# Score products from 32-row or 64-row slices of split q and k, in place of 128-row stacks read back from DRAM

## The reference

```python
# A: 4 heads, each with two components of 32 channels
sc = jnp.einsum("bqhcd,bkhcd->bhcqk", qblk, k).astype(jnp.float32) * scale
sc = jnp.where(kpos[None, :] <= qpos[:, None], sc, -jnp.inf)
p = jax.nn.softmax(sc, axis=-1)
pd = p[:, :, 0] - lam * p[:, :, 1]
# C: 4 heads of 64 channels, dilated windows, here as one softmax with a mask of log counts
sc = jnp.einsum("nbqhd,nbkhd->nbhqk", qb, k2).astype(jnp.float32) * scale
```

## Time and profile before

| | |
|---|---|
| median of three runs | 927.5 us |
| the profiled execution | 927.7 us, span 925.9 us |
| busy: TensorE / VectorE / ScalarE / GpSimd | 698.4 / 506.5 / 337.4 / 285.0 us |
| DMA queue of SyncE | 80.60 MB |
| DMA queue of GpSimd (gathers) | 67.12 MB |
| granted TensorE clock, mean | 0.873 of full speed |

### The profile page before, as it was taken

How to read it: one execution, slowest core, us unless ns; L and a number is a source line. 1 busy time by engine, 2 the same in 40 slices (tenths; PEclk the granted TensorE clock), 3 DMA queues, 4 the chain that set the end, 5 groups by cost and what they waited for, 6 DMA issues and landing times.

```text
span 925.9 us, 11484 instructions
## 1 busy us (share of the span) xinstructions
PE 698.4 (75%) x4171; PEld 565.0 (61%) x4171; DVE 506.5 (55%) x801; ACT 337.4 (36%) x731; POOL 285.0 (31%) x195
## 2 busy tenths in 40 slices
PE   4699999999778995994128750777646359979996
PEld 4599888888667774784014430554535246668885
DVE  5745864553557854343028860696844487665222
ACT  6523232322112122321006820676727366672111
POOL 4034445465345554261005201331131262000000
PEclk9699999999899998898558975889969578999999
DMA  7544678775768878646445423332314261522231
GB/s 233 187 146 136 188 232 272 257 232 172 242 209 282 303 261 286 193 160 237 114 138 171 173 91 129 127 104 67 109 56 151 88 179 49 70 1 94 101 104 69
DMA packets 87277, 148.44 MB, mean 160 GB/s; under 512 B 14131, under 2 KB 57955, under 8 KB 87222
## 3 DMA queue, kind: packets, MB, share of 16 engines
q1 hardware_dynamic: 68790, 80.60, 28.5%
q0 software_dynamic: 18432, 67.12, 21.7%
HBM read 124.47 MB, written 23.26 MB: 160 GB/s over the span
## 4 chain that ended last, share of the span: by engine, by line
PE 40%; DMA 31%; DVE 10%; SPq 6%; issue 5%; ACT 4%; POOL 4%; ACTq 0%; DVEq 0%; POOLq 0%
DMA ka_d<-KL 6%; PE ps L1779 6%; PE ps L1781 5%; PE ps L1780 5%; DMA kc<-in_cache_c_k 4%; DMA kc<-in_w_out 4%; DMA TMP<-gate_d 4%; PE ps L1840 3%; PE ps L1912 3%; PE ps L1913 3%; PE ps L1914 3%; DMA stack<-kc_d 3%; DMA stack<-ka_d 2%; DMA vc<-in_cache_c_v 2%; DMA kbuf<-in_cache_a_k,index 2%
## 5 line engine op out<-in xcount | busy, mean ns | idle before, releaser
L1779 PE MATMUL ps<-xh,wh 128*128 128x344 f32 x576 | 198.1, 344 | 9.1 <-DVE passing L1255 7.1
L1780 PE MATMUL ps<-xl,wh 128*128 128x344 f32 x576 | 188.2, 327 | 0.0
L1781 PE MATMUL ps<-xh,wl 128*128 128x344 f32 x576 | 188.0, 326 | 0.0
L1282 DVE TENSOR_TENSOR prod<-kbuf,qrep 128x1024 f32<-128x1024 f32 x64 | 87.6, 1368 | 86.6 <-DMA kbuf<-in_cache_a_k,index 83.6
L1779 PEld LDWEIGHTS ps<-xh,wh 128*128 128x128 f32 x576 | 112.0, 194 | 31.3 <-issue 21.3
L768 POOL DMA_INDIRECT kbuf<-in_cache_a_k,index x64 | 72.9, 1139 | 138.1 <-DVE sc L1284 131.7
L1780 PEld LDWEIGHTS ps<-xl,wh 128*128 128x128 f32 x576 | 112.4, 195 | 0.0
L1781 PEld LDWEIGHTS ps<-xh,wl 128*128 128x128 f32 x576 | 112.0, 194 | 0.0
L1807 PE MATMUL ps<-stack,stack 128*128 128x512 f32 (+3 forms) x96 | 35.7, 459 | 100.1 <-DMA stack<-ka_d 72.8
L776 POOL DMA_INDIRECT vbuf<-in_cache_a_v,index x64 | 67.6, 1056 | 130.9 <-PE ps L1740 115.8
L1045 ACT ACTIVATE E<-T,negmax 128x128 f32<-128x128 f32 (+7 forms) x96 | 73.6, 768 | 48.2 <-DVE negmax L1404 48.0
(11 more groups left out here) (262 smaller groups left out, 1149.4 us busy)
## 6 DMA issues: line engine op xcount, KB each, us to landing
wraw<-in_w_in SPq DMA_DIRECT2D x24, 512.0 KB, 7.8
gate_d<-passing SPq DMA_DIRECT2D x8, 516.0 KB, 6.8
TMP<-gate_d SPq DMA_DIRECT2D x8, 516.0 KB, 6.5
xraw<-in_x_prompt SPq DMA_DIRECT2D x8, 512.0 KB, 6.1
out<-nat SPq DMA_DIRECT2D x8, 512.0 KB, 5.5
stack<-kc_d SPq DMA_DIRECT2D x8, 512.0 KB
kc<-in_w_out SPq DMA_DIRECT2D x8, 512.0 KB, 11.6
x_res<-in_x_prompt SPq DMA_DIRECT2D x8, 512.0 KB, 4.1
```

Source lines behind the costliest of these rows:

```text
L1282: link(dve.tensor_tensor(prod[:], kbuf[n % 2][:], qrep[b % 2][:].unsqueeze(1).to_broadcast([P, CH, W_BR]), ALU.mult))
L1779: pe.matmul(pr, wh[t % 2][:, kt, :], xh[:, kt, cols], start=(kt == 0), stop=False)
L1780: pe.matmul(pr, wh[t % 2][:, kt, :], xl[:, kt, cols], start=False, stop=False)
L1781: ins = pe.matmul(pr, wl[t % 2][:, kt, :], xh[:, kt, cols], start=False, stop=(kt == KT - 1))
```

## The change

The stacks, their DRAM tensors, the stores and the loads are taken out. A pair's split halves stay in SBUF, and the scores read a head's own rows of them. The first pair keeps QH, QL, KH, KL; the second and fourth share four tiles `half0x`, the third has `half1x`, all where the stacks were. So the split of the second pair waits for the end of the projections (whose inputs lie there), and that of the fourth for the last score of head 3. Each component of an A head and each C head has three accumulated products, qh kh + ql kh + qh kl, over 32 or 64 rows; the product ql kl is left out. For an A unit both PSUM halves are awaited first, and the two components' products alternate. `v_c` is loaded at unit 10 rather than 34.

```diff
-        stack = [[at(f"stack{s}{i}", [P, S], F32R) for i in range(4)] for s in range(2)]
+        halves = [[at(f"half{s}{i}", [P, S], F32R) for i in range(4)] for s in range(2)]
...
+        pair = [[QH, QL, KH, KL], halves[0], halves[1], halves[0]]
...
             for step in range(PSTEPS + 8):
...
-                if step - 10 in SPLIT_AT and SPLIT_AT.index(step - 10) % 2:
-                    store_pair(0, SPLIT_AT.index(step - 10) // 2)
...
             sp.wait_ge(proj, ALL_CHUNKS)
...
-            load_stack(0, 0, FIRST, first_stack)
             sp.dma_start(mask_a[:], a["c_mask_a"]).then_inc(mask_in, 16)
-            load_stack(0, FIRST, S)
             gates_stored(sp)
             sp.dma_start(v_a[:], nat_out["va"]).then_inc(va_in, 16)
-            load_stack(1)
             sp.dma_start(mask_c[:], a["c_mask_c"]).then_inc(late_in, 16)
             for u in range(NU + 1):
                 h, q = UNITS[u] if u < NU else (8, 0)
-                if q == NQ - 1 and h in (0, 2, 4):
-                    store_pair(h // 2 + 1, 0)
-                    store_pair(h // 2 + 1, 1)
-                if q == 1 and h >= 1 and h + 1 < 8:
-                    load_stack(h + 1)
-                if u == UNITS.index((HA, 2)):
-
-                    sp.wait_ge(scored, ITEM_NO["s", UNITS.index((HA, 1)), 0] + 1)
+                if u == UNITS.index((1, 2)):
+
                     sp.wait_ge(split_done, 8)
                     sp.dma_start(v_c[:], nat_out["vc"]).then_inc(vc_nat_in, 16)
...
-                if p >= 1 and i == 0:
-                    pool.wait_ge(qk_out, stored(p - 1))
+                if p == 1 and i == 0:
+
+                    pool.wait_ge(proj, ALL_CHUNKS)
+                if p == 3 and i == 0:
+
+                    pool.wait_ge(scored, ITEM_NO["s", UNITS.index((HA - 1, NQ - 1)), 1] + 1)
...
-                high, low = ((QH, QL), (KH, KL))[i // 2]
+                high, low = pair[p][2 * (i // 2):2 * (i // 2) + 2]
...
-                    act.wait_ge(qk_out, stored(3))
+                    act.wait_ge(split_done, 16)
...
             def scores(u):
...
+                if q == 0 and h % 2 == 0:
+                    pe.wait_ge(split_done, 4 * (h // 2 + 1))
+                qh, ql, kh, kl = pair[h // 2]
+                qs = slice(q * P, (q + 1) * P)
+                n, d = (2, DKA) if h < HA else (1, DHC)
+                for c in range(n):
+                    keep_free(pe, ("s", u, c))
+                for k0 in range(0, w, 512):
+                    k1 = min(w, k0 + 512)
+                    for i, (a_, b_) in enumerate(((qh, kh), (ql, kh), (qh, kl))):
+                        for c in range(n):
+                            r = slice(64 * (h % 2) + d * c, 64 * (h % 2) + d * c + d)
+                            ins = pe.matmul(score_bank(("s", u, c))[:, k0:k1], a_[r, qs], b_[r, k0:k1],
+                                            start=(i == 0), stop=(i == 2))
+                            if i == 2 and k1 == w:
+                                ins.then_inc(scored, 1)
```

More of the change, by code:

```diff
@@ L304, in build @@
         sn_d = dram("sn_d", [2, NB, HCA])
-        qa_d, ka_d = dram("qa_d", [2, 4, 2, DKA, S]), dram("ka_d", [2, 4, 4, DKA, S])
-        qc_d, kc_d = dram("qc_d", [2, 2, 2, DHC, S]), dram("kc_d", [2, 2, P, S])
         x_d, xs_d = a["x_prompt"][0], a["x_sample"].rearrange("b t d -> (b t) d")
@@ L343, in build @@
         misc_out = sem("misc_out")
-        qk_out = sem("qk_out")
-        first_stack = sem("first_stack")
-        stack_in = [sem(f"stack_in{i}") for i in range(2)]
         va_in, vc_nat_in = sem("va_in"), sem("vc_nat_in")
@@ L440, in build @@
         EARLY_MIX = 2
[L441 to L447, removed]
         def keep_free(eng, it):
@@ L554, in _ @@
             sp.dma_start(cs[:, 0:2, :], a["state_conv"][0][:, 1:3, :]).then_inc(misc_out, 16)
[L556 to L567, removed]
             turn_no = [0]
@@ L638, in _ @@
             sp.wait_ge(proj, ALL_CHUNKS)
[L640 to L662, removed]
             def load_wo(k):
@@ L1794, in scores @@
                 w = (q + 1) * P
-                sl = stack[h % 2]
-                if u == 0:
-                    pe.wait_ge(first_stack, 16 * 4)
-                if u == FIRST // P or (q == 0 and h >= 1):
-                    pe.wait_ge(stack_in[h % 2], stacked(h))
-                for c in range(2 if h < HA else 1):
-                    it = ("s", u, c)
-                    keep_free(pe, it)
-                    out = score_bank(it)
-                    for k0 in range(0, w, 512):
-                        k1 = min(w, k0 + 512)
-                        if h < HA:
-                            ins = pe.matmul(out[:, k0:k1], sl[2 * c][:, q * P:(q + 1) * P], sl[2 * c + 1][:, k0:k1],
-                                            start=True, stop=True)
-                        else:
-                            pe.matmul(out[:, k0:k1], sl[0][:, q * P:(q + 1) * P], sl[1][:, k0:k1], start=True, stop=False)
-                            ins = pe.matmul(out[:, k0:k1], sl[0][:, q * P:(q + 1) * P], sl[2][:, k0:k1],
-                                            start=False, stop=True)
-                    ins.then_inc(scored, 1)
+                if q == 0 and h % 2 == 0:
[14 more added lines that the diff above has]
+                                ins.then_inc(scored, 1)
             def turn(u):
```

## The result

The changed kernel takes 836.3 us (median of four runs, 834.7 to 838.4), beside 927.2 us (924.6 to 928.8) for the kernel before on the same chip: a ratio of 0.902, 95% interval 0.899 to 0.906. A median here is of all runs of a kernel, a ratio and its interval of its fast runs alone, without those over 1.5% above its fastest. The forecast was 837 with a range of 806 to 880. The sum came out; its terms did not, and most of what follows is about that. The profiled execution took 834.8 us, with a span of 833.0 against 925.9.

The account below looks back on a forecast made before the run. The prediction saw TensorE 40% and DMA 31% of the wait chain, DMA mostly the split q/k round trip through DRAM, with VectorE binding attention between stalls. 9 + 32 + 31.5 + 10 + 21 - 13 = 90.5 off 927.7 gives 837, range 806 to 880.

Parts of the forecast that it names:

- The wait for vc, 9: End of the projections: without stores queued ahead, vc lands at the median and TensorE's 11.42 us wait goes; gain 9.
- The start, 32: Projections to unit 3: mask_a no longer waits behind KL's store and the first stack; u=3 moves from 487.87 to 456.
- Units 3 to 16, 31.5 less 7: Early A heads: 90.7 us fall to 59.2 at the free pace of 4.55 a unit, before costs of added products.
- Before unit 36, 10: C heads: the 10.14 us idle goes because v_c and a gate load both come earlier; 0 if the gate load stays late.
- Units 43 to 48, 21: C heads: 50.05 us against 19 for five free units; of 31 lost to w_out, a stall of 10 stays.
- The added products, 13: Scores: row slices overlap; exposed cost 3 in A, 6 in C, 4 for the banks; bounds 0 and 66.
- The 4 for the common wait for both banks: A units: the first product waits until VectorE has read both banks of the unit before; cost 4, 24 without cover.
- Row slices: Rival, score products: slices run one after the other, 42 us of TensorE work in place of 16.8; 866 us, chance 0.10.
- this change from slices to full rows: Rival, 64 units: each change of shape drains TensorE, 128 changes of 0.16 us add 20; 857 us, chance 0.08.
- the other transfers: Rival: gate loads and w_out stay late, slowed by the gathers rather than the stacks; 874 us, chance 0.14.
- the signs named as right: Attention: first mask some 15 us after projections, u=16 some 73 and u=32 some 152 after u=0, masks idle only for ScalarE.
- the signs named as wrong: Components over 0.2 us apart, masks mostly awaiting scores, load waits over 10 us, or granted clock near 0.5 through A heads.

Follow-up runs that it names:

- The first experiment: Changed kernel with the two stores of the split q (QH, QL) back on SP's queue ahead of the last vc loads; 858.5 us, ratio 0.923.

## Why the prediction was right, and which of its terms were not

*The wait for vc, 9.* The first experiment shows the mechanism. The stretch gave 15.6: the 11.42 us that TensorE waited are gone, and the other 4.2 lie within the spread of this stage between profiles of the same code. So 9, of at most 11.4, was near. With the round trip left in place it would have been worth 3.2.

*The start, 32.* Mis-sized, 40.1. The prediction kept three times of the trace before, and each fell. The last gate store, at 431.82, waits for VectorE's last step on its tile, and that ended 4.1 us after the last projection product, because VectorE had work on the samples, from 426.94 to 430.33, ahead of its last three steps on the tile; now it ends 2.1 after. The store took 2.56 us to issue, now 0.32. And mask_a lands in 4.16, not 8.2. VectorE's last step on the tile before the change; its like now starts at 413.60:

```profile
431.28 0.51 DVE L1255 SCALAR_TENSOR_TENSOR passing<-passing,ps 128x344 f32<-128x344 f32 x1
```

Thus 7 us from the last projection product to the first mask, where "some 15" was forecast.

*Units 3 to 16, 31.5 less 7.* 25.3 against 24.5, but by luck: both parts were too large. The free pace of 4.55 did not come; 65.5 us are 5.04 a unit, near the 4.96 of heads 2 and 3 that the prediction had as a bound. And the added products do not cost 7 here: without the two products with low halves the stretch takes 65.0. What holds the pace at 5.04 is not settled. The load of v_c ahead of the gate load cost nothing: it landed in 5.5.

*Before unit 36, 10.* The idle time did go, but 3.2 came of it, since unit 34 now takes 12.3 us where it took 5.4. The step that failed is "both come earlier, so 10 goes": it did not ask what the earlier gate load sets in motion. Before, GpSimd waited 20.89 us for that load and began its recurrence step and the split of the fourth pair at 683.57, behind the samples' last steps that stand in unit 34. Now it begins at 583.20, beside them. In units 32 to 36 VectorE runs the same instructions for the same units, and is busy 20.99 us where it was busy 14.13 (rows below); five short ones in unit 34 make up 7.0 of it. The longest of these, before and after, then GpSimd before and after:

```profile
667.54 0.19 DVE L1459 TENSOR_TENSOR w<-us,pT 128x32 f32<-128x32 f32 x1
```
```profile
586.70 2.38 DVE L1402 TENSOR_TENSOR w<-us,pT 128x32 f32<-128x32 f32 x1
```
```profile
683.57 2.37 POOL L848 TENSOR_TENSOR xb<-xb,TMP 128x1024 f32<-128x1024 f32 x1 [20.89 <-DMA TMP<-gate_d]
```
```profile
586.67 2.35 POOL L759 TENSOR_TENSOR half<-qc,half 128x1024 fp32r<-128x1024 f32 x1
```

Unit 34 takes 5.3 us in the kernel before with its stores moved as well, and 11.1 to 12.8 in all the others that have the samples' last steps there. No run keeps GpSimd idle in that unit, so this is read from the traces. Units 32 to 36 and 43 to 48 (length, busy us of PE, PEld, DVE, ACT, POOL, clock, DMA), before and after:

```profile
657.93:685.59 27.66, 11.59 (x70) 9.35 (x69) 14.13 (x35) 9.05 (x21) 5.01 (x2) 0.69 0.31 94
712.11:762.16 50.05, 20.37 (x97) 16.54 (x97) 28.23 (x64) 25.93 (x41) 23.28 (x10) 0.66 0.43 127
```
```profile
575.01:599.49 24.48, 14.50 (x81) 11.71 (x81) 20.99 (x35) 10.52 (x25) 11.77 (x6) 0.80 0.20 65
628.39:664.88 36.49, 24.63 (x105) 18.92 (x105) 29.22 (x64) 24.88 (x41) 24.54 (x10) 0.67 0.44 130
```

*Units 43 to 48, 21.* 13.6. "Five free units are 19" is false: the pace of 3.79 was taken from units 36 to 43, which have none of the samples' last steps, and VectorE alone was busy 28.23 of the 50.05, so no more than 22 could go. "A stall of 10 stays, from w_out's refills" named the wrong wait. The refills land in 3.8 and ScalarE waits 1.4 for them; what stays is VectorE's own work, a good part of it beside GpSimd's.

*The added products, 13.* Too large by some 5, an estimate from the ledger and the run without low products. They overlap and are covered in A, as forecast: there both low products together are worth 1.3. In C they are exposed, 4.3 from unit 48 on and 2.4 in units 36 to 43, where TensorE is now busy 28.88 of 28.90 us; that is 6.7, near the 6 forecast. The 9.7 of the run without low products is another sum, since it takes out two products of three in C, where the change added one to two. The 4 for the common wait for both banks no run prices. (36 x 0.23 is 8.3, not 8.4, and four times that 33.1, not 33.6; nothing hangs on it.)

*The rivals.* Row slices do not run one after the other; the weighted sum of unit 5 starts 0.24 us behind the last pair of slices, which itself takes 0.12, so this change from slices to full rows costs at most 0.12; the other transfers did not stay late. Of the signs named as right, u=16 and u=32 came 78.7 and 156.1 us after u=0, not 73 and 152, and in A masks waited not only for ScalarE (12.7 us in all) but also for score products (8.8, in eight units). Of the signs named as wrong, one was there in part: the granted clock was 0.50, the 1.2 GHz level, from 420 to 435.

So the time was right by luck: errors of 15 and 17 us, of opposite sign, cancelled. The first is mostly a start whose issue and landing times were kept from the trace before. The second has three parts: 7 us that VectorE's short steps in unit 34 lose beside GpSimd, 7 by a pace taken from units without the work of units 43 to 48, and 2.4 of added products that the table books after unit 48.

## What to carry to other kernels

A wait that ends in a stretch is worth at most the length of that stretch less the busiest engine's time in that same stretch; a pace from neighbouring units is no bound where other steps are written between them. It is worth less where the load that comes earlier also sets another engine going: look at what that engine will then run beside. When traffic leaves an in-order queue, forecast every issue and landing behind it anew, also the ones that are not in the chain, and look at what stood just ahead of each load rather than at the volume. Two waits that lie side by side are priced together, or by taking each out of the version that lacks the other.

## What the runs showed of the hardware that was not expected

By the trace, a product in free rows of TensorE starts beside products issued before it that wait for theirs: 0.23 us a pair of 512 columns in either order of issue (rows of unit 11, above). The Trainium skill ("TensorE: Matmul & The Clock Gate", part 3, what overlaps and what doesn't) says that matmuls start and end strictly in the order of issue; these rows differ, and the measurement decides. Whether they also end out of order is open, since ends are modelled in the trace.

Some VectorE instructions that touch a few columns take as long as the GpSimd instruction beside them: the copy of 64x8 took 0.16 us with GpSimd idle and 2.33 beside a subtraction of 2.34 (rows at 660.48 to 660.84, above), the step of 128x32 in unit 34 took 2.38 beside 2.35, where before the change it took 0.19. Not all do. The masks, which read PSUM, take as long beside GpSimd as without (0.68 to 0.69 us for 512 columns), and a reciprocal of 128x1 at 653.33 took 0.16 within a GpSimd instruction of 653.25 to 655.64. The Trainium skill ("SBUF — State Buffer", two separate sides) says that GpSimd and those VectorE instructions that run in a two-port mode or have two inputs in SBUF share a pair of ports as an exclusive lock, held for a whole instruction, and that the one that comes second blocks. These rows agree: the copy started 0.03 us behind the subtraction and ended 0.02 behind it.

After the gap between projections and attention, in which TensorE does little, the granted clock is at 0.50 (1.2 GHz), and it is back at 1.00 (2.4 GHz) at different times in kernels whose code there is the same. Forty us from the first mask on (length, busy us, then clock), in the changed kernel and in the one with paired C heads, whose A heads are the same:

```profile
418.93:458.93 40.00, 32.11 (x199) 19.89 (x199) 30.74 (x63) 22.13 (x55) 14.02 (x10) 0.74 0.32 98
```
```profile
420.48:460.48 40.00, 33.08 (x158) 20.41 (x158) 24.07 (x55) 16.99 (x44) 8.95 (x8) 0.55 0.26 81
```

TensorE is as busy in both and does a fifth fewer products in the second; units 4 to 8 take 29.3 us there and 23.1 in the first. In that with serial components and both banks awaited it was 0.58, with stores of q ahead of vc 0.54. What decides it stays open.
